# A decoder layer on one Trainium2 core: second stick-breaking score pass on all 128 rows, and one fill read ahead of the first head's exponentials

## What is computed

```python
def stick_breaking_attention(q, k, v):
    z = einsum('bhqd,bhkd->bhqk', qb, kb) * HEAD_DIM ** -0.5     # strict causal
    log_one_minus = where(strict, log_sigmoid(-z), 0.0)
    suffix = cumsum(log_one_minus, reverse=True) - log_one_minus
    weights = where(strict, exp(log_sigmoid(z) + suffix), 0.0)
    return weights @ v
def forgetting_attention(q, k, v, cum_log_f):
    z = einsum(q, k) * HEAD_DIM ** -0.5 + cum_log_f[t] - cum_log_f[s]
    return softmax(where(causal, z, -inf)) @ v
def reference(x, ...):            # x: 512 tokens of width 1024
    h = x @ w_in + b_in           # sb q,k,v | fox q,k,v | forget logits | two gates
    y_sb, y_fx = stick_breaking(...) @ w_proj_sb, forgetting(...) @ w_proj_fox   # 8 heads of 64 each
    merged = sigmoid(g_sb) * y_sb + sigmoid(g_fx) * y_fx
    x = layer_norm(ALPHA * x + merged @ w_out)
    u_gate, u_val = split(x @ w_up)                     # 2 x 2816
    return layer_norm(ALPHA * x + (gelu(conv3(u_gate)) * u_val) @ w_down)
```

## Time and profile before

| | |
|---|---|
| time, median of 3 runs | 756.1 us (756.01 to 756.1) |
| profiled execution | 755.87 us, of which the span of instructions is 754.1 us |
| granted clock of TensorE, mean | 0.997 |
| PE busy | 743.7 us, 99% of the span |
| PEld / DVE / ACT / POOL busy | 620.6 / 365.3 / 318.1 / 338.7 us |
| DMA | 78.33 MB, mean 104 GB/s |
| median from issue to landing, a weight load (512 KB) / a stack DMA (128 KB) | 3.3 / 2.3 to 2.4 us |

### The profile page before, as it was taken

The page is one execution under the profiler, slowest core; times in us unless marked ns, Lnnn a source line. Parts: engine busy times, 40 slices in busy tenths (PEclk is TensorE's granted clock), DMA queues, the critical chain, the costliest instruction groups (busy, mean ns, idle before and its releaser), DMA issues.

```text
span 754.1 us, 9599 instructions
## 1 busy us (share of the span) xinstructions
PE 743.7 (99%) x3528; PEld 620.6 (82%) x3528; DVE 365.3 (48%) x506; ACT 318.1 (42%) x429; POOL 338.7 (45%) x245
## 2 busy tenths in 40 slices
PE   9999999999999999999999999999999999999996
PEld 6888788888888888888898888888888888888884
DVE  3339679879789764446552112211221122322567
ACT  4322584774765775662123332323332243423410
POOL 6654254434533424992005445454544453655800
PEclk9999999999999999999999999999999999999998
DMA  8223413314214123761003322222232327332002
GB/s 311 96 98 113 125 37 114 102 56 116 81 56 139 57 84 112 279 223 56 1 1 113 107 88 98 97 91 103 86 109 83 111 83 280 111 110 85 29 29 83
DMA packets 24477, 78.33 MB, mean 104 GB/s; under 512 B 2944, under 2 KB 3328, under 8 KB 24448
## 3 DMA queue, kind: packets, MB, share of 16 engines
q1 hardware_dynamic: 24448, 77.94, 30.8%
HBM read 71.63 MB, written 2.10 MB: 98 GB/s over the span
## 4 chain that ended last, share of the span: by engine, by line
PE 93%; DVE 3%; ACT 1%; issue 1%; DMA 1%; SPq 0%; DVEq 0%; ACTq 0%
PE ps L978 90%; PE ps L1076 2%; DVE sb_t L800 1%; DMA w_raw<-w_stream_in 0%; PE ps L1156 0%; DVE fx_nmax L792 0%; DMA fx_k<-k_bias_rows 0%; ACT fx_p L555 0%; DVE sb_k L757 0%; DVE qk_lo L693 0%; DVE fx_lo L693 0%; DVE sb_t L823 0%; SPq L342 0%; DVE fx_k L693 0%; ACT sb_t L549 0%
## 5 line engine op out<-in xcount | busy, mean ns | idle before, releaser
L414 POOL TENSOR_TENSOR w_lo<-w_raw,w_hi 128x512 fp32r<-128x512 f32 x220 | 295.9, 1368 | 374.0 <-ACT w_hi L476 368.4
L476 ACT ACTIVATE w_hi<-w_raw 128x1024 fp32r<-128x1024 f32 x109 | 115.4, 1060 | 218.6 <-DMA w_raw<-w_stream_in 218.5
L978 PE MATMUL ps<-x1T_hi,w_hi 128*128 128x512 f32 (+1 forms) x376 | 141.3, 376 | 0.0
L978 PE MATMUL ps<-x1T_lo,w_hi 128*128 128x512 f32 (+1 forms) x376 | 141.2, 375 | 0.0
L978 PE MATMUL ps<-x1T_hi,w_lo 128*128 128x512 f32 (+1 forms) x376 | 141.2, 375 | 0.0
L941 DVE SCALAR_TENSOR_TENSOR conv<-ps,col,conv 128x511 f32<-128x511 f32 (+1 forms) x44 | 33.0, 749 | 166.8 <-ACT conv L656 162.5
L978 PE MATMUL ps<-xT_hi,w_hi 128*128 128x512 f32 x264 | 105.9, 401 | 1.2 <-ACT g_all L524 1.2
L978 PE MATMUL ps<-xT_hi,w_lo 128*128 128x512 f32 x264 | 103.2, 391 | 0.0
L978 PE MATMUL ps<-xT_lo,w_hi 128*128 128x512 f32 x264 | 102.9, 390 | 0.0
L978 PEld LDWEIGHTS ps<-x1T_lo,w_hi 128*128 128x128 f32 x376 | 70.8, 188 | 12.9
L978 PEld LDWEIGHTS ps<-x1T_hi,w_hi 128*128 128x128 f32 x376 | 70.8, 188 | 12.9
(11 more groups left out here) (142 smaller groups left out, 1131.9 us busy)
## 6 DMA issues: line engine op xcount, KB each, us to landing
w_raw<-w_stream_in SPq DMA_DIRECT2D x109, 512.0 KB, 3.3
wout_raw<-w_out_in SPq DMA_DIRECT2D x8, 512.0 KB, 5.0
r_raw<-w_stream_in SPq DMA_DIRECT2D x5, 512.0 KB, 10.7
xT_raw<-xT_in SPq DMA_DIRECT2D x8, 256.0 KB, 6.5
x<-x_tok_in SPq DMA_DIRECT2D x4, 512.0 KB, 4.2
ln_rows<-rows_in SPq DMA_DIRECT2D x4, 512.0 KB, 5.7
out_dram<-x SPq DMA_DIRECT2D x8, 256.0 KB, 2.0
sb_q<-sb_q SPq DMA_DIRECT2D x8, 128.0 KB, 2.3
```

The costliest lines, as they stand in the source:

```text
L414: lo = nc.gpsimd.tensor_tensor(w_lo[:, slot, cs], w_raw[:, slot, cs], plain(w_hi[:, slot, cs]), ALU.subtract)
L476: nc.scalar.activation(w_hi[:, slot, :], w_raw[:, slot, :], ACT.Copy).then_inc(hi_ready, 1)
L978: return nc.tensor.matmul(out_, lhs, rhs, start=start, stop=stop, skip_group_check=True)
```

## The change

There are two edits. The first gives the second stick-breaking pass all 128 rows. `qk_lo` is split into `sb_ql[0]`, `sb_ql[1]` (one for each head of the pair) and `k_lo`; a new function `low_stack` copies the 64 rows of q_lo into the other 64 by one DMA a head, so that the pass gives q_lo by (k_hi + k_lo). PE waits for these two DMAs (`lo_stack_in`) between the two passes. For the first pair they follow `stack(0)` at once, for the others they come behind the fourth weight load of the odd step. The second edit moves `fill(0, 0)` of ACT (step 0 alone) ahead of the four exponentials.

```diff
+            def low_stack():
+
+                for e in range(2):
+                    sp.dma_start(plain(sb_ql[e][other_rows(e), :]),
+                                 plain(sb_ql[e][rows_of(e), :])).then_inc(lo_stack_in, 16)
...
                     sp.wait_ge(qk_split, 2)
                     stack(0)
+                    low_stack()
...
+                    if h % 2 == 1 and h < TAIL and k == 3:
+                        low_stack()
...
-                if h > 0:
+                if h == 0:
+                    fill(h, 0)
+                else:
                     act.wait_ge(o_split[1], h)
                 act.wait_ge(fx_maxed, h * SB + SB)
...
-                fill(h, 0)
+                if h > 0:
+                    fill(h, 0)
...
-                    lo = (qk_lo[r, j, :] if j < 2 else q_bias_rows[r, e, :] if j == 2 else fx_k[e][r, :])
+                    lo = (sb_ql[e][r, :], k_lo[r, :], q_bias_rows[r, e, :], fx_k[e][r, :])[j]
...
-                for q, k, first in ((sb_q[e][:], sb_k[e][:], True), (qk_lo[hd, 0, :], sb_k[e][hd, :], False)):
+                for q, k, first in ((sb_q[e][:], sb_k[e][:], True), (sb_ql[e][:], sb_k[e][:], False)):
+                    if not first:
+                        pe.wait_ge(lo_stack_in, (pair + 1) * 32)
```

More of the change, by code:

```diff
@@ L164, in layer @@
     v_all = at("v_all", [P, SB, 1024], f32, area_a)
-    qk_lo = at("qk_lo", [P, 2, SEQ], f32r, area_a + 22 * K)
+    sb_ql = [at("sb_ql0", [P, SEQ], f32r, area_a + 22 * K), at("sb_ql1", [P, SEQ], f32r, area_g + 24 * K)]
+    k_lo = at("k_lo", [P, SEQ], f32r, area_a + 24 * K)
     sb_q = [at("sb_q0", [P, SEQ], f32r, area_a + 16 * K), at("sb_q1", [P, SEQ], f32r, area_a + 18 * K)]
@@ L268, in layer @@
         o_hi_done, o_split = [sem("sb_o_hi"), sem("fx_o_hi")], [sem("sb_o_split"), sem("fx_o_split")]
+        lo_stack_in = sem("lo_stack_in")
         stack_in = [sem("sb_stack_in"), sem("fx_stack_in")]
@@ L339, in stack @@
                     q, k = (sb_q[e], sb_k[e]) if b == 0 else (fx_q[e], fx_k[e])
-                    k_other = qk_lo[own, 1, :] if b == 0 else k_bias_rows[own, e, :]
+                    k_other = k_lo[own, :] if b == 0 else k_bias_rows[own, e, :]
                     sp.dma_start(plain(q[other, :]), plain(q[own, :])).then_inc(stack_in[b], 16)
                     sp.dma_start(plain(k[other, :]), plain(k_other)).then_inc(stack_in[b], 16)
+            def low_stack():
+                for e in range(2):
+                    sp.dma_start(plain(sb_ql[e][other_rows(e), :]),
+                                 plain(sb_ql[e][rows_of(e), :])).then_inc(lo_stack_in, 16)
             for n in range(W_SLOTS, N_PAIR + 3):
```

## The result

The changed kernel takes 762.47 us (median of 6 runs, 761.19 to 764.09), the kernel before 756.0 (6 runs, 755.34 to 756.1): a ratio of 1.0082, 95% interval 1.0072 to 1.0093. It is slower, as forecast, but by 6.5 us instead of 2.85, and so outside the range. The profiled execution of the changed kernel took 762.40 us, its span 760.6 us (before: 755.87 and 754.1), with a mean granted clock of 0.993 instead of 0.997.

A forecast was written before the change was run, and what follows sets the result against it. PE was taken to bound the kernel (busy 743.7 of 754.1 us), following an ACT and DVE chain in step 0. 3.1 + 0.7 + 0.2 - 1.15 = +2.85 us gave 759.0 us, range 756.6 to 761.0.

The forecast's parts named there:

- the chain: Step 0, ACT and DVE from norms to sb_lo: 0.13 us of room, so moving the fill read gains only 0.1 us.
- the scan: Step 0, DVE's last scan beside POOL's w_lo: loses 1.1 us, bounds 0 and 1.3.
- the norms: Step 0, third and fourth norm on DVE beside POOL's v_low: lose 2.1 us, bounds 0 and 2.4.
- the stand of PE: Step 0: PE, through its two eighths at 92.4, stands about 4 us until the transposes.
- what the wider pass saves: Second pass on 128 rows: 0.19 us gained a step, 1.15 us over steps 1, 3, 4, 5, 6 and 7.
- the new DMAs: Low stacks on SP's queue: step 0 moves by +0.2 us; later pairs land some 0.5 us early, no wait.
- the clock: Step 0, behind PE's stand: the granted clock may fall to 1.2 GHz, costing 0.7 us, between 0 and 1.3.
- the low stack of step 0: Pair 0's transfers: 0.35 us wait less 0.19 of the faster pass, +0.2 us (-0.2 to +0.4).
- (d): Rival: clock stays low through step 0, or low stacks late in steps 2, 4, 6; 760 to 761 us, chance 0.10.
- (b): Rival: POOL costs nothing beside step 0's scan and norms; -1.05 us, 755.1 us, chance 0.12.
- (a): Rival: only step 0's norms are held up, not the scans, and the clock holds; +1.05 us, 757.2, chance 0.17.
- (c): Rival: the edits do what their names say, stand and passes gained whole; -3.3 us, 752.8 us, chance 0.03.

The follow-up runs named there:

- x4: x1 with ACT releasing POOL later, so POOL stays away from step 0's scans and norms; 756.45 us, ratio 0.9997 to the kernel before.
- x9: x7 plus the second edit as in x4 (fill read ahead, POOL held off); 754.04 us, ratio 0.9974 to the kernel before.
- x3: The changed kernel with the low stack directly behind stack(0), ahead of the fourth weight load; 760.64 us, ratio 1.0049 to the kernel before.
- x7: Kernel before with the first edit alone, low stack ahead of the fourth load, even steps' first weight load behind the forgetting stack; 753.95 us, ratio 0.9976.
- x8: Kernel before with the first edit alone, low stack still behind the fourth load, even steps' first weight load behind the forgetting stack; 755.22 us, ratio 0.9996.
- x1: Kernel before with the second edit only (fill read and high weights ahead of step 0's exponentials); 761.32 us, ratio 1.0059.
- x10: x1 run once more, on the same chip as x11; 760.02 us, ratio 1.0059 to the kernel before.
- x5: x4 with only its first wait, so POOL is away from the scans but beside the norms; 759.64 us, ratio 1.0055 to the kernel before.
- x6: x1 plus 28 zero-weight matmuls on PE ahead of its step 0 wait for the norms; 759.55 us, ratio 1.0056 to the kernel before.
- x11: x6 run once more, beside x10; 759.9 us, ratio 1.0055 to the kernel before.
- x2: Kernel before with the first edit only (second pass on 128 rows, low stack behind the fourth weight load); 757.86 us, ratio 1.0018.

## Why the prediction was wrong in size

**Right.** The direction; that the second edit brings nothing by itself because the chain has only 0.13 us of room (x4, x9); the scan (1.04 us against 1.1) and the norms (2.01 against 2.1), with POOL's starts at 86.16 and 92.96 where I had 86.3 and, with the scan's delay, near 93; the stand of PE (3.8 us against about 4); what the wider pass saves (0.20 to 0.23 a step against 0.19). The scan's row was the unknown: no row of before had a scan beside POOL. DVE's scan ends 1.08 us after POOL's instruction (88.61 against 87.53), so it stood until POOL was over and then ran. The rule of the Trainium skill that I had weighed there ("SBUF — State Buffer", section "Who interferes with whom") holds in this trace for a scan as well; it would have had the scan lose what was left of POOL's instruction, 1.16 us (1.37 less the 0.21 by which POOL was ahead), and the trace has 1.04.

**The step that failed** is the one on the new DMAs: "For the later pairs the load issued just ahead lands after its usual 3.3 us or a little more and each stack DMA about 0.5 behind it … no wait, but with little room". The low stacks took up to 5.0 us and PE waited 0.34, 0.93 and 0.92 us for them. I had put it at nothing, and had the gain of the pass in steps 4 and 6 besides; for all steps behind the first my sum had -1.15 and the trace has +1.7 (-0.9 in the odd steps, +2.1 in the even ones, +0.5 at the forgetting scores behind them). By the traces that is 2.85 of the 3.65 us by which I missed; the clock is 1.3 more, the low stack of step 0 with the gap between its passes 0.4 less, and scan and norms 0.1 less. The fault was in the reading: I took the weight loads' median of 3.3 us from a page over the whole kernel, while the earlier trace rows had a stack DMA that was issued behind a load, and it took 4.3 (the three ahead of it, behind the same load, took 4.3 to 4.5). In the changed kernel a load is also issued behind it, at 189.57, before it lands. x3, x7 and x8 show the cause: without the load ahead the median landing is 2.5 and at most 0.2 us of wait is left, and without the load behind it is 3.9 with 0.2 of wait. My rival (d) named "a low stack comes late in steps 2, 4 and 6 as well", but gave it a chance of 0.10 together with the clock and a price of 1 to 2 us. It happened in all three steps and together with the clock, on top of the forecast's own terms: 4.15 us (2.85 and 1.3), so that the time passed the 761 of (d) too.

**Mis-sized: the clock.** I took 0.7 of a range of 0 to 1.3. In the profiled execution it cost 2.0, since the clock was low until about 101.3, for the first transposes and the seven weight matmuls behind them; PE, not the chain, was then the late one (`sb_hi` of ACT waits 1.71 us for PE's transposes of `sb_t`). My bound came from the 3.6 us that PE took for its first eight matmuls, and nothing said that a low stretch is always that long: here they were 3.4 to 6.8 us. What its share is in the medians stays open.

**Wrong with little weight:** in step 0 the low stack was in time, so -0.2 and not +0.2. Two sums were off as well. The gain of the passes has 6 x 0.24 = 1.44 as its upper end, not 1.7. And the forecast's own range of 757.9 to 760.0 is narrower than its bounds: with clock, scan and passes all at their ends the terms give 756.6 to 760.3. The measured 762.5 lies outside either.

**Rivals.** (b), that POOL costs nothing, was decided where I put it, at the order of starts, and x4 is that case: 0.9997 with POOL held off. (a) fell with the scan's 2.24 us. (c) fell with x4.

## What to carry to other kernels

An instruction that is moved ahead on one engine brings forward what it releases on others: before moving it, list those instructions and look which ones will then run beside the engine at the front of the chain. A small transfer that a step needs soon belongs ahead of the large loads in its queue, and the large load that follows can be moved behind the next small one; its landing is to be read from a row where it had a load for a neighbour, not from a median. And an edit that takes away a wait is worth only the room of the chain that comes behind it.

## What the runs showed of the hardware

- A scan on DVE with both inputs in SBUF stands beside POOL as other such instructions do: 2.24 us instead of 1.20 when POOL began 0.21 ahead. It holds the other way too: POOL's two `w_lo` instructions took 3.54 us together in x1 beside the scan, and 2.55 in x4 away from it. The maxima, whose input is in PSUM, kept their time (1.65 us for four against 1.66) though POOL worked beside them until 89.70, into the fourth.
- Two short DVE instructions beside two of POOL took 1.42 and 1.48 us instead of 0.41 and 0.48, and each ended 0.2 to 0.3 us behind one of POOL's. POOL lost little there: 2.66 us for its two, 2.54 before.
- The same stand of 3.8 to 3.9 us lowered the granted clock to 1.2 GHz in three executions, for 6.8, 6.8 and 3.4 us (the changed kernel, x1 and x10). A stand of 2.8 us (x5) and one of 0.8 with PE kept busy ahead of it (x6, x11) left it at 2.4 GHz in the profiled executions.
- A DMA of 128 KB from SBUF to SBUF landed after 2.2 to 2.4 us with no load near it. For the low stacks of the later pairs it was 4.0 to 5.0 with a load of 512 KB issued ahead of them and one behind (the changed kernel, x2), 3.8 to 4.3 with one ahead alone (x8), and 2.3 to 3.4 with loads behind alone (x3, x7).
